# Gate slabs set between the branch-gate slabs, an early clear of a block matrix, and a last remainder on VectorE

## The reference, cut to what matters

```
mod = silu(c) @ ada_w + ada_b ; shift, scale, gate = split(mod, 3)
h = rms_norm(x) * (1 + scale) + shift ; p = h @ w_in     # ..., g_a, g_b are columns of p
merged = sigmoid(g_a) * br_a + sigmoid(g_b) * br_b
x = x + gate * (merged @ w_o)
```

## Time and profile before

| | before |
|---|---|
| median of three runs | 1236.59 us (1235.32 to 1241.18) |
| profiled execution: its time is its span | 1237.0 us |
| busy: PE, PEld | 1167.1 us (94%), 984.1 us (80%) |
| busy: POOL, ACT, DVE | 923.3 us (75%), 595.4 us (48%), 464.7 us (38%) |
| chain that ended last | PE 65%, POOL 18%, issue 6%, DVE 5%, ACT 4% |

### The profile page before, as it was taken

One profiled execution on the slowest core, in us unless ns is written; L12 is line 12 of the kernel. 1 busy time (PEld: TensorE's weight loads), 2 busy tenths in 40 slices (PEclk: granted clock), 3 DMA queues, 4 the chain that ended last, 5 costly groups with the idle time before them and its releaser, 6 DMA issues.

```text
span 1237.0 us, 21229 instructions
## 1 busy us (share of the span) xinstructions
PE 1167.1 (94%) x8406; PEld 984.1 (80%) x8406; DVE 464.7 (38%) x801; ACT 595.4 (48%) x866; POOL 923.3 (75%) x927
## 2 busy tenths in 40 slices
PE   7999899999898999999999999999899989999997
PEld 7899798687687888788988887877777977888785
DVE  5627655754554111102435566433234233111101
ACT  6464433434555445535554545655355436445533
POOL 4688954431397888786899998679897757888784
PEclk9999999999999999999999999999999989999999
DMA  9987432332264666565565544355565525665562
GB/s 322 291 262 203 129 87 87 119 105 87 84 221 142 201 179 187 164 198 159 140 170 146 143 138 137 115 156 159 202 238 170 154 68 164 194 184 183 163 200 87
DMA packets 182898, 202.10 MB, mean 163 GB/s; under 512 B 7528, under 2 KB 141072, under 8 KB 182032
## 3 DMA queue, kind: packets, MB, share of 16 engines
q1 hardware_dynamic: 177584, 185.78, 50.0%
q10 hardware_dynamic: 5216, 14.97, 3.6%
HBM read 196.51 MB, written 4.21 MB: 162 GB/s over the span
## 4 chain that ended last, share of the span: by engine, by line
PE 65%; POOL 18%; issue 6%; DVE 5%; ACT 4%; DMA 1%; POOLq 0%; ACTq 0%; DVEq 0%
POOL wlo L2643 18%; PE ps L694 18%; PE ps L696 17%; PE ps L695 17%; PE ps L691 11%; PE ps L699 2%; ACT whi L1301 1%; DVE x L1872 1%; DMA raw<-in_w_in 1%; ACT L1301 1%; ACT rl L1301 0%; DVE tmp L1869 0%; DVE hE L1864 0%; DVE gt L1864 0%; DVE kkn L1872 0%
## 5 line engine op out<-in xcount | busy, mean ns | idle before, releaser
L2643 POOL TENSOR_TENSOR wlo<-raw,whi 128x256 fp32r<-128x256 f32 (+1 forms) x918 | 917.8, 1034 | 298.2 <-ACT whi L1301 297.0
L1301 ACT ACTIVATE whi<-raw 128x1024 fp32r<-128x1024 f32 x324 | 340.5, 1056 | 308.6 <-PE ps L696 271.6
L694 PE MATMUL ps<-whi,hThi 128*128 128x512 f32 (+1 forms) x656 | 264.2, 403 | 15.7 <-POOL wlo L2643 8.9
L696 PE MATMUL ps<-whi,hTlo 128*128 128x512 f32 (+1 forms) x656 | 255.6, 390 | 0.0
L695 PE MATMUL ps<-wlo,hThi 128*128 128x512 f32 (+1 forms) x656 | 255.1, 389 | 0.0
L694 PE MATMUL ps<-hThi,whi 128*128 128x256 f32 x568 | 167.6, 295 | 11.9 <-issue 4.7
L695 PE MATMUL ps<-hTlo,whi 128*128 128x256 f32 x568 | 162.4, 286 | 0.0
L694 PEld LDWEIGHTS ps<-whi,hThi 128*128 128x128 f32 x656 | 123.6, 188 | 48.7 <-issue 21.1
L696 PE MATMUL ps<-hThi,wlo 128*128 128x256 f32 x568 | 162.3, 286 | 0.0
L696 PEld LDWEIGHTS ps<-whi,hTlo 128*128 128x128 f32 x656 | 123.7, 189 | 26.5
L695 PEld LDWEIGHTS ps<-wlo,hThi 128*128 128x128 f32 x656 | 123.9, 189 | 21.8
(11 more groups left out here) (385 smaller groups left out, 1544.4 us busy)
## 6 DMA issues: line engine op xcount, KB each, us to landing
raw<-in_w_in SPq DMA_DIRECT2D x120, 512.0 KB, 3.8
raw<-in_ffn_w_in SPq DMA_DIRECT2D x176, 256.0 KB, 3.1
raw<-in_ffn_w_down SPq DMA_DIRECT2D x44, 512.0 KB, 4.2
raw<-in_w_mkv SPq DMA_DIRECT2D x16, 512.0 KB, 6.2
raw<-in_ada_w SPq DMA_DIRECT2D x8, 512.0 KB, 6.0
raw<-in_w_o SPq DMA_DIRECT2D x8, 512.0 KB, 4.2
raw<-in_w_branch_a SPq DMA_DIRECT2D x8, 512.0 KB, 3.7
raw<-in_w_branch_b SPq DMA_DIRECT2D x8, 512.0 KB, 3.7
```

What stands on the lines that cost most here:

```text
L694: e.matmul(o, l[0], r[0], start=start, stop=False)
L696: return e.matmul(o, l[1], r[0], start=False, stop=stop)
L1301: return e.activation(o, i, f, **k)
L2643: p = e.tensor_tensor(wlo[c % NHL][:, o], raw[i % NRAW][:, o], whi[c % NHL][:, o], ALU.subtract)
```

## The change

There are three edits. The gate slabs no longer stand in pairs behind each group g(n): `tm` gets a table `behind` of what to put behind a slab, and a(n).0 now stands behind g(n).1, a(n).1 behind g(n).3. The sum `gatesum n-1` moves from behind g(n).3 to behind g(n).0. The chains are still finished before g3.2, which is now behind a3.0. The memset of `AD` moves on POOL to the point where the row of the first feed-forward layer is loaded (`load f1`, behind the last wo slab). And the remainder of the very last slab is left out by POOL, made by DVE in one piece ahead of the first quarter of the tail, and signalled by a semaphore of its own, `lo_v`.

```diff
+    def tm(self, grp, w, cols, ev, arg, lhs="h", gen=0, nk=8, behind={}):
...
             self.unit("tm", self.slab(parts, (2, o)), grp, ev, arg, lhs, gen, kh=kh, nk=nk, last=kh == nk // 2 - 1)
+            if kh in behind:
+                behind[kh]()
...
         for n in range(4):
-            tm(f"g{n}", w, [(3912 + 512 * n, 512)], "gate1", n)
+            behind = {1: lambda n=n: gate(n, 0), 3: lambda n=n: gate(n, 1)}
             if n:
-                do("gatesum", n - 1)
-            for kh in range(2):
-                ... (the gate slab and its unit, now in gate(n, kh))
+                behind[0] = lambda n=n: do("gatesum", n - 1)
+            tm(f"g{n}", w, [(3912 + 512 * n, 512)], "gate1", n, behind=behind)
...
+        last_slab = plan.split[-1]
...
-                w.wait_ge(S["lo"], i)
+                w.wait_ge(S["lo_v" if i == last_slab else "lo"], i)
...
+                if u.kind == "tail" and half == 0:
+                    last_remainder()
...
+            def last_remainder():                       # on DVE
+                c = place[last_slab]
+                w.wait_ge(S["hi"], last_slab)
+                w.wait_ge(S["mm"], ("use", plan.split[c - NHL]))
+                tt(wlo[c % NHL][:, :], raw[last_slab % NRAW][:, :], whi[c % NHL][:, :], ALU.subtract).then_inc(
+                    S["lo_v"].tick(last_slab), 1)
...
+                    if i == last_slab:                  # on POOL
+                        ahead[0] += 1
+                        continue
...
-            def hgrn():
+            def hgrn_zero():
                 e.memset(AD[:, :, :, :], 0.0).then_inc(S["hg_g"].tick("zero"), 1)
-                for _ in range(59):
-                    yield
...
+                elif what == "load" and d[0] == "f1":
+                    hgrn_zero()
```

More of the change, by code:

```diff
@@ L199, in fm @@
         return i
-    def tm(self, grp, w, cols, ev, arg, lhs="h", gen=0, nk=8):
+    def tm(self, grp, w, cols, ev, arg, lhs="h", gen=0, nk=8, behind={}):
         for kh in range(nk // 2):
@@ L290, in build, with gate @@
         do("open", "dsa", 99)
+        def gate(n, kh):
+            i = self.slab([(None, ada[512 * kh:512 * kh + 512, 2048 + 256 * n:2304 + 256 * n]
+                            .rearrange("(k p) n -> p k n", p=P))], (4, 256), True)
+            self.unit("gate", i, f"a{n}", "gate", n, kh=kh, last=kh == 1)
         for n in range(4):
-            tm(f"g{n}", w, [(3912 + 512 * n, 512)], "gate1", n)
+            behind = {1: lambda n=n: gate(n, 0), 3: lambda n=n: gate(n, 1)}
             if n:
-                do("gatesum", n - 1)
-            for kh in range(2):
-                i = self.slab([(None, ada[512 * kh:512 * kh + 512, 2048 + 256 * n:2304 + 256 * n]
-                                .rearrange("(k p) n -> p k n", p=P))], (4, 256), True)
-                self.unit("gate", i, f"a{n}", "gate", n, kh=kh, last=kh == 1)
+                behind[0] = lambda n=n: do("gatesum", n - 1)
+            tm(f"g{n}", w, [(3912 + 512 * n, 512)], "gate1", n, behind=behind)
         self.before("g3", 2, ("finish", "rwkv", "head0", "head1"), ("split", "ya"))
@@ L455, in lay_out @@
         return order
-SIGNALS = ["vecs", "const", "small", "bias_out", "hk", "row", "final", "mem0", "mem1", "mem_k", "mem_x", "k_out", "m_out", "con", "out", "hi", "lo", "mm", "ev_v", "ev_a", "lhs",
+SIGNALS = ["vecs", "const", "small", "bias_out", "hk", "row", "final", "mem0", "mem1", "mem_k", "mem_x", "k_out", "m_out", "con", "out", "hi", "lo", "lo_v", "mm", "ev_v", "ev_a", "lhs",
            "ada", "pre_pe", "pre_v", "pre_a", "split_a", "post_v", "post_a", "turn_pe",
@@ L2655, in head @@
                     yield
-            def hgrn():
+            def hgrn_zero():
                 e.memset(AD[:, :, :, :], 0.0).then_inc(S["hg_g"].tick("zero"), 1)
-                for _ in range(59):
-                    yield
-            chains = {"head0": head(0), "head1": head(1), "hgrn": hgrn()}
+            chains = {"head0": head(0), "head1": head(1)}
             for what, *d in order:
```

## The result

The changed kernel takes 1252.25 us (median of four runs, 1246.65 to 1255.42), the kernel before 1238.88 on the same chip (1235.32 to 1245.95): a ratio of 1.0088, 95% interval 1.0053 to 1.0122. Timed again beside the later experiments (e12) it came to 1.0057 (1.0032 to 1.0081). The forecast of 1230.0 and its whole range are wrong, and the sign is wrong.

What follows compares the result with a forecast made beforehand. PE, busy 94% of the span, and POOL's remainders, 18% of the last chain, were taken as the bound. 2.2 + 3.3 + 1.1 = 6.6 us off span 1237.0 gives 1230.4, forecast 1230.0; own range 1228.5 to 1231.5, wider 1226.0 to 1237.5.

Steps and rivals of the forecast that it cites:

- The other moves of this edit I cost at nothing.: Gate stage: other buffer waits, moved sums, a3.0's new place, DVE's adds and SP's loads were taken to cost nothing.
- Only the tail counts: Rival: moved chain steps make the gate stage lose what the memset gives; 1235.5 us, chance 0.09.
- Gate slabs, 2.2 us: Gate stage at g1.2: stop splits into two shorter waits and the clock stays up; 2.2 us back, bounds 0.5 to 4.15.
- The waiting sums: slower: Rival in the gate stage: each `gatesum` waits for ACT's copy, three stops of 4.15 us; 1240.5 us, chance 0.09.
- Memset, 3.3 us: At 642 us: moving it shrinks PE's stop by 1.8 us and lifts the clock; 3.3 us taken, bounds 0 to 3.8.
- The clock's part: Behind the memset's stop: low clock goes with the stop, 1.6 us taken of 1.7 at most.
- The rival by the lock rule: Rival at the memset: scans shut out remainders in its place, so moving it gives 0; 1233.3 us, chance 0.04.
- Its new place: Memset before the first feed-forward norm: fits POOL's 5.88 us wait for ACT, costs nothing; 1.81 without that gap.
- Last remainder, 1.1 us: Tail, slab 21: DVE makes the remainder in 1.28 us, so PE starts 1.1 us earlier.
- The sum: Whole kernel: gate slabs 2.2, memset 3.3 and last remainder 1.1 together give 6.6 us.
- The chance of 0.08 for slower: Whole kernel: chance 0.08 of slower than 1242.8 us, from an ACT lag no row shows and unforeseen mishaps.

Runs made afterwards that it cites:

- e12: The changed kernel, all three edits, timed once more against the kernel before: ratio 1.0057.
- e4: The kernel before with only its chain steps placed where the changed kernel has them; slabs, gate bursts and sums in old order: 1248.4 us, 1.0087.
- e3: The changed kernel, all three edits, but with chain steps left between the same half slabs as in the kernel before: 1233.34 us, 0.9959.
- e1: The changed kernel without its first edit: gate stage as before, memset early, last remainder on DVE: 1236.94 us, 0.997 of the kernel before.
- e8: The kernel before, with head1 allowed no more than 34 steps until the finish of the heads starts: 1252.04 us, 1.0095.
- e10: e3 with the last attention projection's product left in PSUM for the residual add: 1233.03 us, 0.9964 of the kernel before.
- e2: The kernel before with the first edit alone (gate slabs and sums moved); memset and last remainder as before: 1254.95 us, 1.0107.
- e7: The changed kernel, with head1's chain told to have 34 steps done before g3.0 and 36 before g3.1: 1250.1 us, 1.0084 of the kernel before.
- e14: The changed kernel, with dsa stopped ahead of its first softmax step until the heads are finished: 1243.31 us, 1.0047 of the kernel before.

## Why the prediction was wrong, point by point

- **The step that failed** is "The other moves of this edit I cost at nothing." I listed what moves by the lines of the diff: slabs, sums, one slab across the finish. The list is the planner's input, and the chain steps of two heads and dsa moved with it. That they might stood in one rival, "Only the tail counts", at what the memset gives, 3.3 us, and a chance of 0.09, with no look at which steps. By e4, with no slab moved, it costs 10.8 us by the ratio, 8.2 by the medians and 9.4 in the trace of the stage. Which of the moved steps cost it stays open.
- **Gate slabs, 2.2 us.** The sum assumed the stream around g1.2 as it was. The reload was late as computed, but a chain step stood behind its rounding, and the stop became 2.95 us with the lower clock behind it. With the steps in place (e3), PE's stop is 1.86 us and the clock is 1.00 from 225 to 250 us. What the new slab order gives is 1.4 us by the ratios (e3's less e1's, 0.0011), well within the intervals: right in sign at most.
- **The waiting sums: slower.** Right in sign, wrong in mechanism. `gatesum 0`, `1` and `2` started at 226.65, 248.47 and 284.78 us behind no wait. ACT's lag at a0 came from the same chain steps, and they had moved.
- **Memset, 3.3 us: mis-sized, 1.7 measured.** The stop shrank by 0.6, not 1.8: POOL now stands idle for 1.13 us in front of the remainder at 655.41, waiting for ACT's `whi`. The memset had filled that time; 1.8 less 1.13 is what was left. The clock's part came out in size, as against this one profile of the kernel before, but partly by luck: the sum took the low clock as a consequence of the memset, and e4 and e8 keep the memset and the 2.02 us and don't have the low clock. The rival by the lock rule (0) was wrong too: twelve remainders ran in 10.76 us beside the scans.
- **Its new place** at nothing: right (idle for 7.35 us behind it).
- **Last remainder, 1.1 us:** 1.2 measured, with 1.23 us for DVE's instruction where I took 1.28.
- **The sum** of 6.6 us would have been near for the kernel that I had in mind: e3 gives 5.1 (interval 2.2 to 8.1). But e3's traces show that it isn't made up as the sum was: the gate stage is 0.5 us shorter in e3 and 0.5 longer in e10, where the sum had 2.2. The chance of 0.08 for slower was too small for an edit of a planner's input.

## What to carry to other kernels

If a planner or a scheduler works out the order of work, a diff of its input isn't a diff of the program: lay both orders side by side and follow every step that changes its neighbours, the small ones above all. Where chains are finished without cover, the order of small instructions on in-order queues can be worth more than a late slab: a copy that slipped behind a softmax made PE wait for 3.8 us, and 8 us at half speed followed. A low clock in one profile is not yet the price of the stop in front of it: look whether the same stop has it in other profiles. And keep an edit that moves slabs apart from one that moves steps; the two can be applied and timed separately, as e3 and e4 show.

## What the runs showed of the hardware that I had not expected

A DVE instruction with two SBUF inputs can be held up by a whole run of POOL instructions, and not only by the one that it meets. It took 14.43, 14.42, 14.42, 14.62 and 14.58 us (changed kernel, the same in e12, e2, e7, e8), each time ending 0.6 us after POOL's unbroken run of remainders did. Beside such a run it took 1.24 us in the kernel before and in e4, 1.29 in e1, 1.23 in e3 and 0.72 in e14; with one input in PSUM it took 0.69. The Trainium skill, "SBUF — State Buffer", section "SBUF: two separate sides", says that whichever instruction starts first gets the shared port pair for its whole length; the trace agrees that a PSUM operand escapes it, but by that rule DVE would get its turn after one remainder of some 0.7 us, and it waited for about twenty. Why it got a turn in five kernels and not in the other four, no run here tells.
